# Down weights of the two convolution-hosting feed-forward stages split in two fp32r halves

## The chip, the cores and the metric

The kernel runs on one core of a Trainium2 chip, as one program. The metric is the device time of one execution in microseconds. A core has a matrix engine (TensorE, PE in the profile; PEld is its weight load), three engines for elementwise work (VectorE is DVE, ScalarE is ACT, GpSimd is POOL), and a queue that only starts transfers (SyncE, SP). Each engine works through its own list in order, and they meet at semaphores. "Start to start" is the time from the start of one instruction to the start of the next on the same engine; an instruction's own duration is a little longer, since neighbours overlap by 0.08 us.

## The reference

Two blocks in sequence on 256 tokens of width 1024, in fp32. The first has a mixer (gated linear attention and block attention), then a feed-forward layer whose depthwise convolution of three taps is causal. The second has two layers on a latent and a context sequence of 256 tokens each, modulated by projections of a condition vector: a conformer convolution of 31 taps with layer norm, and window attention. Each is followed by a feed-forward layer of this form:

```python
def conv_ffn(h, w_up, w_dw, b_dw, w_down):      # w_up 1024 x 5632, w_down 2816 x 1024
    u = dwconv(h @ w_up, w_dw, b_dw)            # three taps
    a, b = jnp.split(u, 2, axis=-1)
    return (jax.nn.silu(a) * b) @ w_down
...
    v = a * jax.nn.sigmoid(g)                   # conformer_conv
    v = dwconv(v, w_dw, b_dw)                   # 31 taps
    v = jax.nn.silu(layernorm(v, ln_g, ln_b))
    return v @ w_pw2 + b_pw2
```

## The kernel before

All weights lie in HBM as slabs of 128 x 2048 fp32 (1 MB), in the order of their use. A ring of three buffers `raw` takes them in; slab c is in slot c modulo 3, and since the order in a feed-forward stage repeats every three slabs, each of its three kinds keeps one slot. A product in nearly full precision is made of three fp32r matmuls (`mm3`, lines 1706 to 1708): the upper half of the weights `whi` with the upper and the lower half of the activations, and the lower half `wlo` with the upper half of the activations. For that, each slab is split:

- ScalarE writes `whi` as a copy of `raw` (`hi`, line 777). It waits until the slab has landed and until TensorE is through with the slab that last used the slot.
- VectorE and GpSimd write `wlo = raw - whi` together (`lo`, lines 1171 and 735). `pool_words` gives GpSimd's part: the last 512 columns in the stages of `DOWN_WHOLE`, else the last 1024. VectorE takes the rest.
- The next load into the slot waits for both parts.

Slabs that are kept `whole` skip this. TensorE reads them from `raw` as fp32 (line 626 for down weights, 1776 for the modulation), and the next load into the slot waits for TensorE. Before the change these are the modulation slabs and the down weights of `ffn0` and `ffn_ctx`.

There are four feed-forward stages: `ffn0`, `ffn_ctx`, `ffn_lat`, `ffn2`. Each walks over 11 blocks of 256 inner features (j = 0 to 10, called pairs here, for the pair of tap buffers). For each, TensorE does two up slabs, for the two halves of u (`features`), and one down slab for block j - 1 (`down`). For block j ScalarE applies the middle tap with the bias out of PSUM (`tap`, line 457) and silu (477). VectorE adds the other two taps out of PSUM (line 540, four instructions a half) and multiplies the halves (559, 512 columns). Where down weights are split, ScalarE then copies the product to `m_hi` (487) and VectorE subtracts `m_lo` (568), 512 columns each, before `down`.

`ffn0` and `ffn_ctx` host the 31-tap convolution of the conformer layer between these steps (`host`). ScalarE makes products of one tap with all eight tiles (871, 128 x 2048 in eight instructions, into `bufA` and `bufB` by turns), VectorE adds each to `acc`, which is the tile `sra` (1296, 128 x 2048), and does one tap in each block itself (1303, eight instructions). Blocks 2 to 7 have three products and one own tap each, blocks 0 and 1 two products and one own tap, block 8 the last addition. The layer norm follows in blocks 8 to 10.

The list of a block on VectorE is: lower half of the first up slab of block j + 1, taps of the first half, host step 0, lower half of the second up slab, taps of the second half, host step 1, multiplication, host step 2, and, where split, lower half of down slab j and m_lo. The end of each stage is drawn apart: behind down slab 9 stand three modulation slabs, then the last down slab (`ffn0_end` and the like), which goes to the slot of the first modulation slab and can be loaded only after that one is used. Then `outputs` waits for its banks, and VectorE adds them to the residual (1376, 1392 and 1550).

Of the kernel before, what the change touches and what calls it, by code (L numbers as in the profile page):

```python
# [31 lines left out]
RING = 3  # L32
# [137 lines left out]
PROCESSING = processing()  # L170


DOWN_WHOLE = {"ffn0", "ffn_ctx"}


def kept_whole():

    out = []
    for use, i in KEYS:
# [3 lines left out]
        elif use.startswith("ada"):  # L183
            out.append(True)
        elif ffn in DOWN_WHOLE:
            out.append(use != ffn or (i >= 4 and i % 3 == 1))
# [8 lines left out]

def pool_words(use):

    return 512 if use.removesuffix("_end") in DOWN_WHOLE else 1024


class Slab:
# [58 lines left out]
def build(nc, io):  # L260
# [16 lines left out]
    with ctx:  # L277
# [146 lines left out]
        def down_slab(b0, j):  # L424

            return b0 + 3 * j + 4
# [9 lines left out]
        def split_ffn(use):  # L436

            return [u for u in ("ffn0", "ffn_ctx", "ffn_lat", "ffn2") if u not in DOWN_WHOLE].index(use) if use not in DOWN_WHOLE else None

        def ffn_v(f):  # L440
            return (0, 1, 1, 2)[f]
# [4 lines left out]
        def ffn_act(act, hi, f, use, tail=None, host=None):  # L446

            b0, whole, fs = BASE[use], use in DOWN_WHOLE, split_ffn(use)
            centre = 2 if f == 0 else 1
            c, b = COL[f"ffn_w{ffn_v(f)}"][0] + centre * 2 * FT, COL[f"ffn_b{ffn_v(f)}"][0]  # L450

            def tap(half, j, par):

                buf = (cva, cvb)[half]
                for m in range(2):
                    t = 2 * j + (m + half * FT)
                    ins = act.activation(buf[:, par, m, :], ps[:, 2 * par + half, m * T:m * T + T], ACT.Identity,  # L457
                                         scale=cols[:, bass.ds(t + c, 1)], bias=cols[:, bass.ds(t + b, 1)])
                ins.then_inc(tap0, 1)

            def up(g, j, par, first):
                hi(g + RING)
                act.wait_ge(slab_done, g.number() + 1)
                if not first:
                    act.wait_ge(mid_f, j + (f * NJ - 1))
                tap(0, j, par)
                if host:
                    host(j, par, 0)
                hi(g + (RING + 1))
                act.wait_ge(slab_done, g.number() + 2)  # L470
                if not first and not whole:
                    act.wait_ge(mid_lo, j + (fs * NJ - 1))
                tap(1, j, par)
                if host:
                    host(j, par, 1)
                act.wait_ge(conv_out, 2 * j + (f * 2 * NJ + 1))
                act.activation(cva[:, par, :, :], cva[:, par, :, :], ACT.Silu).then_inc(silu_done, 1)
                if host:
                    host(j, par, 2)

            def split(j, par, first):
                if whole:
                    return
                act.wait_ge(mid_f, j + (f * NJ + 1))
                if not first:
                    act.wait_ge(slab_done, down_slab(b0, j - 2) + 1)
                act.activation(m_hi[:, par, :, :], cvb[:, par, :, :], ACT.Copy).then_inc(mid_hi, 1)

            up(Slab(b0), 0, 0, True)
            split(0, 0, True)  # L490
            up(Slab(b0 + 2), 1, 1, True)
            hi(Slab(b0 + 4 + RING))
            split(1, 1, True)
            if host:
                with act.Fori(0, 3) as jj:
                    for u in range(2):
                        up(Slab(b0 + 5 + 3 * u, 2, jj), 2 * jj + (2 + u), u, False)
                for j in (NJ - 3, NJ - 2):
                    up(Slab(b0 + 3 * j - 1), j, j % 2, False)
            else:  # L500
                with act.Fori(0, 4) as jj:
                    for u in range(2):
                        g = Slab(b0 + 5 + 3 * u, 2, jj)
                        up(g, 2 * jj + (2 + u), u, False)
                        hi(g + (2 + RING))
                        split(2 * jj + (2 + u), u, False)
            g = Slab(b0 + 3 * NJ - 4)
            up(g, NJ - 1, 0, False)
            others = BASE[use + "_end"] - BASE[use] - COUNT[use]
            hi(g + (2 + RING))  # L510
            if others == RING:
                hi(g + (3 + RING))
            split(NJ - 1, 0, False)
            for k in range(1 if others == RING else 0, others):
                hi(g + (3 + k + RING))
            if tail:
                tail()
            hi(g + (3 + others + RING))
            return g.c + 3 + others + RING + 1


        def ffn_dve(dve, lo, order, f, use, host=None, tail=None):

            b0, whole, fs = BASE[use], use in DOWN_WHOLE, split_ffn(use)

# [69 lines left out]
        def ffn_pe(pe, features, mm3, f, use, x, split, free, early=None, before_down=None, before_end=None, host=None):  # L595


            b0, whole, fs = BASE[use], use in DOWN_WHOLE, split_ffn(use)

# [122 lines left out]
        def _(pool):  # L722
# [4 lines left out]
            def run(c, use, k0, k1):  # L727

                part = slice(SLAB - pool_words(use), SLAB)

                def lo(g):
                    if g.whole:
                        return
                    pool.wait_ge(hi_done, g.split() + 1)
                    pool.tensor_tensor(wlo[:, g.slot, part], raw[:, g.slot, part], whi[:, g.slot, part].bitcast(F32),  # L735
                                       ALU.subtract).then_inc(lo2_done, 1)

                while k0 < k1 and not steady(c + k0, c + k1):
                    lo(Slab(c + k0))
                    k0 += 1  # L740
                times = (k1 - k0) // RING
                if times > 1:
                    with pool.Fori(0, times) as j:
                        for k in range(RING):
                            lo(Slab(c + k0 + k, 1, j))
                    k0 += RING * times
                for k in range(k0, k1):
                    lo(Slab(c + k))
# [18 lines left out]
        def _(act):  # L767
# [272 lines left out]
            def squares_after(q, x, ready):  # L1040
# [4 lines left out]
                return tail  # L1045

            c = ffn_act(act, hi, 0, "ffn0", squares_after(0, xlat, 4), conv_act(0, h_hi))


# [11 lines left out]
            gate_bias(1, xlat, 5 * KT)  # L1061
            pw1_act(1, PLACE["pw1_lat", 2], 5, xctx, ctx_sq, ctx_y, h_hi, shift_of(0, 3, 1), (x_ready, 12))
            c = ffn_act(act, hi, 1, "ffn_ctx", squares_after(1, xctx, 12), conv_act(1, g_hi))


# [14 lines left out]
            group_rows("ada_b")  # L1080
            c = hi_to(c, "ffn_lat", 2)
            c = ffn_act(act, hi, 2, "ffn_lat", lambda: squares(xlat, bufB, preload=True, ready=20))


# [77 lines left out]
        def _(dve):  # L1162
            order = Tally(dve_order)

            def lo(g):

                if isinstance(g.j, int) and g.c >= TOTAL or g.whole:
                    return
                part = slice(0, SLAB - pool_words(use_of(g.c)))
                dve.wait_ge(hi_done, g.split() + 1)  # L1170
                dve.tensor_tensor(wlo[:, g.slot, part], raw[:, g.slot, part], whi[:, g.slot, part].bitcast(F32), ALU.subtract)\  # L1171
                   .then_inc(lo_done, 1)
# [1090 lines left out]
```

## Time and profile before

| | |
|---|---|
| median of 3 runs | 1545.44 us (1545.22 to 1550.87) |
| profiled execution, first to last instruction | 1542.9 us, 2.5 us less than the median; the page gives no other time of it |
| TensorE busy | 1435.2 us, 93% |
| VectorE busy | 1006.8 us, 65% |
| ScalarE busy | 823.3 us, 53% |
| GpSimd busy | 580.9 us, 38% |
| mean granted TensorE clock | 0.968 of full speed |
| HBM read | 269.73 MB, 176 GB/s over the span |

The busy shares are means over stages with different limits. The two stages that the change touches run from about 377 to 592 us (`ffn0`) and from about 683 to 898 us (`ffn_ctx`). A busy TensorE includes the overlap of neighbouring matmuls, so its share says that it never rested, not that each matmul was at its shortest.

### The profile page before, as it was taken

The page shows a single profiled execution, that of the slowest core. Times are in us where ns is not written, and L with a number is a line of the kernel's source. Part 1 is how long each engine was busy: PE and PEld are TensorE (multiplying, and loading weights), DVE is VectorE, ACT ScalarE, POOL GpSimd, SP SyncE. Part 2 cuts the span into 40 slices and gives each one's busy share as a digit, 9 for nine tenths or more (in the row PEclk, how much of TensorE's full clock was granted, in tenths as well). Part 3 has the DMA queues.
Part 4 walks back from the last instruction along what each step waited for, and adds up shares of the span by engine and source line. Part 5 has one row for each costly group of instructions (what it writes and reads, how often), then busy time and mean ns, then how long its engine had stood idle before and what let it go on. Part 6 is the DMA issues. An engine that isn't in the chain of part 4 may idle for free.

```text
span 1542.9 us, 27912 instructions
## 1 busy us (share of the span) xinstructions
PE 1435.2 (93%) x11026; PEld 1325.8 (86%) x11026; DVE 1006.8 (65%) x1299; ACT 823.3 (53%) x1155; POOL 580.9 (38%) x192
## 2 busy tenths in 40 slices
PE   5999999899999999899999988999977998699996
PEld 3898879899999987799999878999966767599996
DVE  4322534747899967678999667666656763666666
ACT  3633454445888653558886545545523453355452
POOL 2443335355332213442222144565523300355662
PEclk9999999999999999999999989999988899899998
DMA  7775564345344446542444465555445300454550
GB/s 288 274 281 191 217 246 164 133 169 193 120 164 167 182 171 272 218 164 110 175 181 184 171 227 194 183 186 190 175 165 199 117 0 29 180 202 171 183 190 28
DMA packets 39142, 272.05 MB, mean 176 GB/s; under 512 B 4437, under 2 KB 5589, under 8 KB 6415
## 3 DMA queue, kind: packets, MB, share of 16 engines
q1 hardware_dynamic: 39054, 270.81, 47.2%
q8 instruction: 65, 1.06, 0.3%
q14 instruction: 23, 0.18, 0.0%
HBM read 269.73 MB, written 1.06 MB: 176 GB/s over the span
## 4 chain that ended last, share of the span: by engine, by line
PE 82%; DVE 8%; ACT 3%; DMA 3%; issue 2%; POOL 1%; SPq 0%; DVEq 0%; ACTq 0%; POOLq 0%
PE ps L1706 22%; PE ps L1707 21%; PE ps L1708 21%; PE ps L626 10%; DMA raw<-w_dram 3%; PE ps L1776 2%; DVE rstd L1180 2%; ACT whi L777 2%; PE ps L2068 1%; PE ps L2080 1%; DVE wlo L1171 1%; DVE h_lo L1220 1%; POOL wlo L735 1%; PE ps L1742 1%; DMA mv<-b_forget_dram 1%
## 5 line engine op out<-in xcount | busy, mean ns | idle before, releaser
L735 POOL TENSOR_TENSOR wlo<-raw,whi 128x1024 fp32r<-128x1024 f32 (+1 forms) x183 | 578.6, 3164 | 935.3 <-ACT whi L777 935.3
L777 ACT ACTIVATE whi<-raw 128x2048 fp32r<-128x2048 f32 x183 | 349.4, 1911 | 501.8 <-PE ps L1708 307.2
L1171 DVE TENSOR_TENSOR wlo<-raw,whi 128x1024 fp32r<-128x1024 f32 (+1 forms) x183 | 275.7, 1507 | 383.6 <-ACT whi L777 382.5
L1706 PE MATMUL ps<-h_hi,whi 128*128 128x256 f32 x1320 | 383.7, 291 | 23.0 <-DVE h_lo L1220 17.4
L1707 PE MATMUL ps<-h_lo,whi 128*128 128x256 f32 x1320 | 377.2, 286 | 0.0
L1708 PE MATMUL ps<-h_hi,wlo 128*128 128x256 f32 x1320 | 376.9, 285 | 0.0
L1706 PE MATMUL ps<-g_hi,whi 128*128 128x256 f32 x1088 | 313.6, 288 | 9.1 <-DVE g_lo L1220 2.5
L1707 PE MATMUL ps<-g_lo,whi 128*128 128x256 f32 x1088 | 309.5, 284 | 0.0
L1708 PE MATMUL ps<-g_hi,wlo 128*128 128x256 f32 x1088 | 309.4, 284 | 0.0
L1706 PEld LDWEIGHTS ps<-h_hi,whi 128*128 128x128 f32 x1320 | 256.3, 194 | 35.1 <-issue 29.1
L1707 PEld LDWEIGHTS ps<-h_lo,whi 128*128 128x128 f32 x1320 | 256.8, 195 | 0.4
L1708 PEld LDWEIGHTS ps<-h_hi,wlo 128*128 128x128 f32 x1320 | 256.7, 194 | 0.0
L1706 PEld LDWEIGHTS ps<-g_hi,whi 128*128 128x128 f32 x1088 | 210.3, 193 | 13.5 <-issue 5.0
L1707 PEld LDWEIGHTS ps<-g_lo,whi 128*128 128x128 f32 x1088 | 210.3, 193 | 0.4
L1708 PEld LDWEIGHTS ps<-g_hi,wlo 128*128 128x128 f32 x1088 | 210.1, 193 | 0.0
L626 PE MATMUL ps<-cvb,raw 128*128 128x256 f32 x704 | 160.8, 388 | 2.0 <-DMA raw<-w_dram 2.0
L626 PEld LDWEIGHTS ps<-cvb,raw 128*128 128x128 f32 x704 | 135.9, 195 | 21.9 <-DMA raw<-w_dram 3.3
L1706 PE MATMUL ps<-m_hi,whi 128*128 128x256 f32 x384 | 109.8, 286 | 9.3 <-DVE m_lo L568 9.3
L1707 PE MATMUL ps<-m_lo,whi 128*128 128x256 f32 x384 | 109.6, 285 | 0.0
L1708 PE MATMUL ps<-m_hi,wlo 128*128 128x256 f32 x384 | 109.5, 285 | 0.0
L540 DVE SCALAR_TENSOR_TENSOR cvb<-ps,cols,cvb 128x255 f32<-128x255 f32 (+1 forms) x176 | 76.6, 477 | 14.9 <-ACT cvb L457 10.3
L540 DVE SCALAR_TENSOR_TENSOR cva<-ps,cols,cva 128x255 f32<-128x255 f32 (+1 forms) x176 | 76.7, 477 | 10.9 <-ACT cva L457 6.2
(237 smaller groups left out, 1891.6 us busy)
## 6 DMA issues: line engine op xcount, KB each, us to landing
raw<-w_dram SPq DMA_DIRECT2D x253, 1024.0 KB, 4.9
xlat<-xT_dram SPq DMA_DIRECT2D x1, 1024.0 KB, 4.9
brev<-bias_rows SPq DMA_DIRECT2D x1, 1024.0 KB, 8.8
brev<-ctxT_dram SPq DMA_DIRECT2D x1, 1024.0 KB, 8.9
out_dram<-xlat SPq DMA_DIRECT2D x4, 256.0 KB, 2.5
cols<-cols_dram SPq DMA_DIRECT2D x1, 512.0 KB, 5.7
gates<-tables_dram SPq DMA_DIRECT2D x1, 448.0 KB, 5.7
consts<-consts_dram SPq DMA_DIRECT2D x1, 192.0 KB, 10.3
```

The costliest lines, as they stand in the source:

```text
L540: ins = dve.scalar_tensor_tensor(out, ps[:, 2 * par + half, m * T + src:m * T + src + n], w, out, ALU.mult, ALU.add)
L626: ins = pe.matmul(ps[:, 4 + m // 2, (m % 2) * T:(m % 2) * T + T], wf[:, k, m * P:m * P + P], cvb[:, par, k, :], start=(first and k == 0 an ...
L735: pool.tensor_tensor(wlo[:, g.slot, part], raw[:, g.slot, part], whi[:, g.slot, part].bitcast(F32), ALU.subtract).then_inc(lo2_done, 1)
L777: act.activation(whi[:, g.slot, :], raw[:, g.slot, :], ACT.Copy).then_inc(hi_done, 1)
L1171: dve.tensor_tensor(wlo[:, g.slot, part], raw[:, g.slot, part], whi[:, g.slot, part].bitcast(F32), ALU.subtract)\
L1180: dve.tensor_reduce(rstd[:, i, :], sq[:, 1024 * i:1024 * i + 1024].rearrange("p (t n) -> p n t", n=T), AX.X, ALU.add)\
L1220: ins = dve.scalar_tensor_tensor(out[1][:, m, :], y[:, m * T:m * T + T], shift(m), out[0][:, m, :].bitcast(F32), ALU.add, ALU.subtract)
L1706: pe.matmul(out, w[0], x[0], start=start, stop=False, skip_group_check=True)
L1707: pe.matmul(out, w[0], x[1], start=False, stop=False, skip_group_check=True)
L1708: return pe.matmul(out, w[1], x[0], start=False, stop=stop, skip_group_check=True)
L1742: ins = pe.matmul(ps[:, bank, 0:T], ones[:, :], s, start=(i == 0), stop=(i == len(sums) - 1))
L1776: ins = pe.matmul(ps[r:r + QUAD, bank, 0:SLABC], cnd[:, c:c + QUAD], w[:, t, :], start=(t < 4 and k == 0), stop=(t >= 4 and k == n - 1), s ...
```

## The change

`DOWN_WHOLE` becomes empty. Then `whole` is false for the down slabs of `ffn0` and `ffn_ctx`; ScalarE, VectorE and GpSimd split them as in the other two stages, `down` takes its three-matmul branch, m_hi and m_lo are made there too, and loads into these slots wait for the two lower halves and no more for TensorE. `pool_words` is 1024 for every slab. In ScalarE's loop of the hosting stages the upper half of the down slab and m_hi (`split`) are put behind the host's last step of each block. VectorE's and TensorE's functions have the split branch already.

```diff
-DOWN_WHOLE = {"ffn0", "ffn_ctx"}
+DOWN_WHOLE = set()
...
 def pool_words(use):
 
-    return 512 if use.removesuffix("_end") in DOWN_WHOLE else 1024
+    return 1024
...
             if host:
                 with act.Fori(0, 3) as jj:
                     for u in range(2):
-                        up(Slab(b0 + 5 + 3 * u, 2, jj), 2 * jj + (2 + u), u, False)
+                        g = Slab(b0 + 5 + 3 * u, 2, jj)
+                        up(g, 2 * jj + (2 + u), u, False)
+                        hi(g + (2 + RING))
+                        split(2 * jj + (2 + u), u, False)
                 for j in (NJ - 3, NJ - 2):
-                    up(Slab(b0 + 3 * j - 1), j, j % 2, False)
+                    g = Slab(b0 + 3 * j - 1)
+                    up(g, j, j % 2, False)
+                    hi(g + (2 + RING))
+                    split(j, j % 2, False)
```

## Rows read from the trace of the kernel before

**Rows 1.** Page: busy by engine; shares of the chain that ended last.

```profile
PE 1435.2 (93%) x11026; PEld 1325.8 (86%) x11026; DVE 1006.8 (65%) x1299; ACT 823.3 (53%) x1155; POOL 580.9 (38%) x192
...
PE 82%; DVE 8%; ACT 3%; DMA 3%; issue 2%; POOL 1%; SPq 0%; DVEq 0%; ACTq 0%; POOLq 0%
PE ps L1706 22%; PE ps L1707 21%; PE ps L1708 21%; PE ps L626 10%; DMA raw<-w_dram 3%; PE ps L1776 2%; DVE rstd L1180 2%; ACT whi L777 2%; PE ps L2068 1%; PE ps L2080 1%; DVE wlo L1171 1%; DVE h_lo L1220 1%; POOL wlo L735 1%; PE ps L1742 1%; DMA mv<-b_forget_dram 1%
```

**Rows 2.** Groups by form: count, busy us, mean ns of one, idle before.

```profile
L777 ACT ACTIVATE whi<-raw 128x2048 fp32r<-128x2048 f32 x183 | 349.4, 1911 | 501.8 <-PE ps L1708 307.2 <-DMA raw<-w_dram 194.5
...
L626 PE MATMUL ps<-cvb,raw 128*128 128x256 f32 x704 | 160.8, 388 | 2.0 <-DMA raw<-w_dram 2.0
...
L568 DVE TENSOR_TENSOR m_lo<-cvb,m_hi 128x512 fp32r<-128x512 f32 x22 | 56.9, 2587 | 2.1 <-ACT m_hi L487 2.1
...
L487 ACT ACTIVATE m_hi<-cvb 128x512 fp32r<-128x512 f32 x22 | 13.6, 618 | 4.6 <-DVE cvb L559 4.6
```

**Rows 3.** Windows of one pair: ffn0, ffn_ctx, ffn_lat; length, busy by engine, clock, DMA.

```profile
437.20:455.61 18.41, 18.41 (x129) 17.59 (x129) 17.44 (x23) 15.81 (x33) 5.77 (x3) 1.00 0.43 171
780.16:798.57 18.41, 18.41 (x129) 17.59 (x129) 17.85 (x23) 15.26 (x31) 4.18 (x3) 1.00 0.44 171
1000.00:1017.28 17.28, 17.28 (x146) 17.28 (x146) 10.71 (x14) 8.60 (x9) 10.33 (x4) 1.00 0.51 183
```

**Rows 4.** Timeline of one pair in ffn0, VectorE, then GpSimd: start, us, instruction, idle before.

```profile
490.53 1.76 DVE L1171 TENSOR_TENSOR wlo<-raw,whi 128x1536 fp32r<-128x1536 f32 x1 [0.29 <-ACT whi L777]
492.20 1.88 DVE L540 SCALAR_TENSOR_TENSOR cva<-ps,cols,cva 128x254 f32<-128x254 f32 x4
494.00 2.28 DVE L1296 TENSOR_TENSOR sra<-sra,bufB 128x2048 f32<-128x2048 f32 x1
496.42 1.76 DVE L1171 TENSOR_TENSOR wlo<-raw,whi 128x1536 fp32r<-128x1536 f32 x1
...
505.64 0.68 DVE L559 TENSOR_TENSOR cvb<-cva,cvb 128x512 f32<-128x512 f32 x1
506.24 2.28 DVE L1296 TENSOR_TENSOR sra<-sra,bufB 128x2048 f32<-128x2048 f32 x1
508.82 1.76 DVE L1171 TENSOR_TENSOR wlo<-raw,whi 128x1536 fp32r<-128x1536 f32 x1 [0.30 <-ACT whi L777]
...
490.57 2.86 POOL L735 TENSOR_TENSOR wlo<-raw,whi 128x512 fp32r<-128x512 f32 x1 [9.53 <-ACT whi L777]
```

**Rows 5.** Timeline at a down slab of ffn_lat, VectorE, then GpSimd.

```profile
1014.44 1.23 DVE L1171 TENSOR_TENSOR wlo<-raw,whi 128x1024 fp32r<-128x1024 f32 x1 [1.72 <-ACT whi L777]
1015.59 2.89 DVE L568 TENSOR_TENSOR m_lo<-cvb,m_hi 128x512 fp32r<-128x512 f32 x1
...
1014.49 3.44 POOL L735 TENSOR_TENSOR wlo<-raw,whi 128x1024 fp32r<-128x1024 f32 x1 [2.31 <-ACT whi L777]
```

**Rows 6.** Timeline at a first up slab of ffn_ctx, VectorE, then GpSimd.

```profile
758.37 2.28 DVE L1296 TENSOR_TENSOR sra<-sra,bufA 128x2048 f32<-128x2048 f32 x1
760.57 1.75 DVE L1171 TENSOR_TENSOR wlo<-raw,whi 128x1536 fp32r<-128x1536 f32 x1
...
759.88 3.57 POOL L735 TENSOR_TENSOR wlo<-raw,whi 128x512 fp32r<-128x512 f32 x1 [8.41 <-ACT whi L777]
```

**Rows 7.** Chain that ended last: one down slab and the end of ffn0.

```profile
400.37 6.91 PE ps L626 x32
...
575.34 7.12 DMA raw<-w_dram
...
582.51 9.18 PE ps L626 x32
```

**Rows 8.** Timeline of the end of ffn_lat, ScalarE, then VectorE.

```profile
1139.38 1.91 ACT L777 ACTIVATE whi<-raw 128x2048 fp32r<-128x2048 f32 x1 [10.14 <-DMA raw<-w_dram]
...
1142.47 2.83 DVE L568 TENSOR_TENSOR m_lo<-cvb,m_hi 128x512 fp32r<-128x512 f32 x1
...
1153.38 0.88 DVE L1392 SCALAR_TENSOR_TENSOR xlat<-ps,mod,xlat 128x256 f32<-128x256 f32 x2 [0.56 <-PE ps L1708]
```

## The prediction

> **What bounds the kernel now.** I began with the busy shares and the chain that ended last [rows 1]: TensorE is 93% busy and 82% of the chain, so in most stages a saving in its work shows in the time, unless another engine is about as full. The table by groups gives the two prices that the change swaps [rows 2]: a down slab kept whole runs as 704 / 22 = 32 matmul instructions, and in the chain each slab stands as one piece of 6.91 us [rows 7]; a split slab is 48 matmuls. Windows one period long show the stage as a whole [rows 3]. In ffn0 and ffn_ctx a pair (two up slabs and one down slab) takes 18.41 us, in ffn_lat, where all slabs are split, 17.28. TensorE is full in all three windows, so a split down slab costs 17.28 / 3 = 5.76 us, 1.15 less than 6.91. The same rows carry the warning: VectorE is busy 10.7 us of 17.28 in ffn_lat, but 17.44 and 17.85 us of 18.41 in the stages that host the convolution. There two engines are full. The convolution's additions make the difference, and the change puts more work on just that engine.
>
> VectorE's queue over one pair is listed in [rows 4]: from one first subtraction (490.53) to the next (508.82) 18.29 us. It waits twice for ScalarE's upper half. A queue without waits starts an instruction 0.08 us before the last one ends; measured so the waits are 0.38 and 0.22 us. 17.7 us are work, and no rest of note is left.
>
> **The change part by part.** *TensorE*: minus 1.15 us for each of 22 down slabs, 25 us busy in all, if nothing else sets the pace.
>
> *ScalarE*: one more slab copy, 1.8 us from start to start, and one more m_hi copy, about 0.55 us, on 15.8 busy us per pair [rows 2, 3]: 18.2 us. That is above the 17.28 that TensorE would like, below what VectorE comes to, and it costs nothing beside it.
>
> *VectorE*: the subtraction of 1536 columns takes 1.67 us of its queue (490.53 to 492.20), that of 1024 takes 1.15 (1014.44 to 1015.59) [rows 4, 5]. Two of the first, 3.34, become three of the second, 3.45. The m_lo subtraction of 512 columns is new: 0.60, the place that the multiplication of the same shape takes between 505.64 and 506.24. 17.7 + 0.1 + 0.6 = 18.4 us, with no wait for anyone.
>
> *GpSimd*: two subtractions of 512 columns become three of 1024. It has the time (three in ffn_lat are 10.33 busy us of 17.28 [rows 3]). What matters is what it does to VectorE. In [rows 5] both begin a subtraction at 1014.44 and 1014.49. VectorE ends at 1015.67 and GpSimd at 1017.93, that is 2.26 us later; where m_lo is behind, it stands as 2.89 us, where the multiplication of the same shape takes 0.68, and ends 0.55 us after GpSimd. So the two take turns when both read two operands of SBUF: 512 columns on GpSimd hold VectorE off for some 1.14 us (490.57 + 2.86 less 492.29), 1024 for 2.26. The tap accumulation is free of this. It reads PSUM, and it runs at its normal 1.88 us while GpSimd works [rows 4]. Today both GpSimd pieces, 1.14 us each, disappear wholly under the 1.80 us of taps. With 1024 columns each overhangs: 2.26 + 0.09 - 1.80 = 0.55 us that the addition behind the taps must wait, 1.1 for two. The third piece, that of the down slab, has no taps behind it but an m_lo, as in ffn_lat. Whoever it falls on, VectorE stands still about 2.3 us. 18.4 + 1.1 + 2.3 = 21.8 us per pair.
>
> That holds if the three pieces find the two tap windows. If one of the two misses it (the additions are 2.2 us each, three in a pair, and a piece that meets an addition's end takes the next 2.3 us), it is 18.4 + 2 x 2.3 + 0.55 = 23.6. Between them the order at each hand-over decides, and the trace shows both answers. In [rows 5] GpSimd waited and got the next turn, ahead of m_lo. In [rows 6] GpSimd asked at 759.88, the addition ended at 760.65, and VectorE's next subtraction went first all the same: 3.57 us instead of 2.86. The Trainium skill ("SBUF — State Buffer", Who interferes with whom) says that a VectorE instruction with two SBUF inputs and a GpSimd instruction that reads SBUF exclude each other for the whole instruction, and that issue order decides who blocks. By that order GpSimd would have had its turn at 760.65, and the pair would go to the 23.6 side; the row contradicts it once VectorE has a run of such instructions behind it. I take the middle, 22.7 us, 4.3 more than 18.41.
>
> *How many pairs*: a stage has 11. Pairs 2 to 7 have the full load (three additions, one own tap): 6 x 4.3 = 26 us, by the ends 20 to 31. Pairs 0 and 1 have fewer additions (one and two) beside an own tap: VectorE's list for pair 1 is 18.4 - 2.2 + 2.9 to 5.2 = 19 to 21 us, and pair 0 starts behind the first taps: I take 4.5 us for both. Pairs 8 to 10 have one addition and the layer norm, VectorE rests there today, and TensorE's shorter down slabs count at last: 3 x 1.15 = 3.5 us at most, of which I take 1, for they begin with VectorE behind. Three loads of the next mod slabs and the short waits between are unchanged.
>
> *The end of the stage*: the last down slab's load waits for the mod slab before it and lands 7.12 us after TensorE has nothing else to do; TensorE then starts at once and takes 9.18 us instead of 6.91 after the pause [rows 7]. Split, it needs the upper half, the lower half and m_lo first. ffn_lat shows just this: from the start of the upper half (1139.38, at landing) over m_lo to the last output drained 1153.38, 14.0 us [rows 8]. 14.0 - 9.2 = 4.8 us; the end in ffn_ctx looks alike and I take 4.5 for each.
>
> *What moves otherwise*: a raw slab of down weights is now freed when its halves are made and not when TensorE is through, so loads come earlier. Each is hidden: at 171 to 183 GB/s the queues have room [rows 3]. m_hi and m_lo are free, two pairs apart. The number of bytes is the same.
>
> *Sum*: 4.5 + 26 - 1 + 4.5 = 34 us per stage, 68 for two; by the ends 28 and 39, 56 to 78. The profiled span is 1542.9 us, 2.5 under the median of 1545.44, and the difference is carried over as it is. TensorE would stand still some 5 us in each pair; before, it was slower after a pause (9.18 for 6.91). In the loop it has that time to spare, at the pairs behind I add 1 us. **1545 + 69 = 1614 us.**
>
> **The rivals.**
> *TensorE's saving wins (faster).* VectorE would have to do its pair in 17.3 us. Then 10 x 1.15 = 11.5 us less and 4.5 more at the end of each stage: 1531 us. For it: TensorE is the larger share of the chain, and VectorE rests in pairs 8 to 10. Against: the queue alone is 18.4 us, and the subtractions stand in it in front of work that TensorE waits for, so it can fall behind by one pair only. It decides from the point where VectorE and GpSimd overlap wholly and some 1.1 us of VectorE's list goes.
> *The engines overlap after all.* If GpSimd held VectorE off only where it does now, the pair is 18.4 to 18.8 us. The period stays, the ends cost 4.5 and pairs 0 to 7 up to 3: 1545 + 9 to 15 = about 1557 us. Against it speak all m_lo in ffn_lat and ffn2, 2.6 us in the mean [rows 2].
> *No window is found.* All three pieces fall on additions or subtractions: 18.4 + 6.9 = 25.3 us per pair, 6 x 6.9 = 41 us, with 4.5 + 4.5 and 1 for the two first pairs about 51 per stage: 1647 us. For it: once VectorE is late, upper halves are ready long before it comes to them, and GpSimd starts when it likes.
> *TensorE slows with its pauses* so far that it sets the pace again. At the stretch that [rows 7] show after a pause it takes 9.18 / 6.91 = 1.33 times as long; a whole pair so is 17.28 x 1.33 = 23.0 us, inside the forecast's own span, and only a longer slow stretch would lie above it. It is in the upper tail.
>
> **How the numbers follow.** The forecast (VectorE and GpSimd by turns, one or two pieces uncovered) 0.81; no window or a slow TensorE 0.10; overlap after all 0.06; TensorE's saving 0.03. The forecast's own range is 1601 to 1625; with late starts of the pairs, the hand-overs and a part of the upper rival 1592 to 1640. About 0.5%, 8 us, is what a measurement of this kernel can tell from no change: faster 0.03, same 0.02, slower 0.95.
>
> **What would show it.** In the pairs 2 to 7: 21.8 to 23.6 us from one first subtraction to the next, TensorE busy 17.3 of them, with its waits put down to VectorE's m_lo or GpSimd's wlo; the additions behind the taps longer than 2.28 us. m_lo far above 0.68 us in all four stages. 205 instead of 183 subtractions on GpSimd, all of 1024 columns. About 14 us from the landing of the end slab to its last output. A pair of 17.3 us in ffn0 would make the prediction wrong at its root; one of 18.5 would say that the turns cost nothing; one of 25 that no window is found. A period of ScalarE without rest would mean that I blamed the wrong engine.

## The result and the profile after

The change made the kernel slower: 1593.35 us median (1589.06 to 1595.71, 4 runs) against 1548.02 us of the kernel before beside it, ratio 1.0298 with a 95% interval of 1.0277 to 1.0319. The profiled execution has a span of 1587.3 us, 44.4 more than 1542.9. The forecast was 1614 us, with a range of 1592 to 1640: the right way and mechanism, but half as large again as the growth that came, 69 us against 45. Line numbers behind the changed function are 6 higher (1706 is 1712, 1296 is 1302).

The page, where it answers to [rows 1]: busy time by engine, then the chain that ended last.

```profile
PE 1424.8 (90%) x11378; PEld 1336.2 (84%) x11378; DVE 1081.2 (68%) x1343; ACT 873.8 (55%) x1199; POOL 720.7 (45%) x214
...
PE 61%; DVE 12%; issue 11%; ACT 8%; POOL 4%; DMA 2%; ACTq 1%; SPq 0%; DVEq 0%; POOLq 0%
```

TensorE is busy 10 us less and its share of the chain falls from 82% to 61%. What came in its place are VectorE, ScalarE and GpSimd, and "issue", from 2% to 11%, which is time for which the profile names no wait. The groups by form, which answer to [rows 2]: count, busy us and mean ns, idle before and who ended it.

```profile
L741 POOL TENSOR_TENSOR wlo<-raw,whi 128x1024 fp32r<-128x1024 f32 x205 | 718.4, 3512 | 840.0 <-ACT whi L783 840.0
...
L1712 PE MATMUL ps<-m_hi,whi 128*128 128x256 f32 x736 | 219.3, 298 | 75.2 <-DVE m_lo L574 36.1 <-POOL wlo L741 31.8 <-issue 7.3
...
L574 DVE TENSOR_TENSOR m_lo<-cvb,m_hi 128x512 fp32r<-128x512 f32 x44 | 76.3, 1734 | 3.5 <-ACT m_hi L487 3.5
```

TensorE's waits stand before the first matmul of a down slab, for m_lo and for GpSimd's lower half, 75.2 us in all. In windows of one period, one in ffn0 and one in ffn_ctx, which answer to [rows 3]:

```profile
484.65:506.00 21.35, 17.50 (x126) 17.33 (x125) 20.78 (x26) 18.01 (x34) 13.78 (x4) 0.84 0.42 147
791.90:813.25 21.35, 19.79 (x166) 19.59 (x165) 20.79 (x25) 17.95 (x34) 13.78 (x4) 1.00 0.42 147
```

A pair now takes 21.35 us. VectorE is full (20.8; the rest are its own 0.27 us between an addition and the own tap, and 0.14 us twice between taps). ScalarE is busy 18.0, near the 18.2 of the forecast. TensorE rests before each down slab; the two windows cut its work at different places, so its 17.5 and 19.8 us are not its share of a pair. In the first window it waited 3.85 us before the down slab and took 8.39 us for it, and the granted clock is 0.84 in the mean; in the second the wait was 1.56 us, the slab took 6.01, and the clock stayed at 1.00. VectorE's queue over one pair, under it one row of ScalarE, then GpSimd's, answer to [rows 4]:

```profile
502.01 0.69 DVE L565 TENSOR_TENSOR cvb<-cva,cvb 128x512 f32<-128x512 f32 x1
502.62 2.29 DVE L1302 TENSOR_TENSOR sra<-sra,bufA 128x2048 f32<-128x2048 f32 x1
504.82 1.22 DVE L1177 TENSOR_TENSOR wlo<-raw,whi 128x1024 fp32r<-128x1024 f32 x1
505.95 0.69 DVE L574 TENSOR_TENSOR m_lo<-cvb,m_hi 128x512 fp32r<-128x512 f32 x1
506.56 1.22 DVE L1177 TENSOR_TENSOR wlo<-raw,whi 128x1024 fp32r<-128x1024 f32 x1
507.69 1.89 DVE L546 SCALAR_TENSOR_TENSOR cva<-ps,cols,cva 128x254 f32<-128x254 f32 x4
509.50 2.67 DVE L1302 TENSOR_TENSOR sra<-sra,bufB 128x2048 f32<-128x2048 f32 x1
512.17 3.34 DVE L1177 TENSOR_TENSOR wlo<-raw,whi 128x1024 fp32r<-128x1024 f32 x1
515.44 1.88 DVE L546 SCALAR_TENSOR_TENSOR cvb<-ps,cols,cvb 128x254 f32<-128x254 f32 x4
517.23 2.70 DVE L1302 TENSOR_TENSOR sra<-sra,bufA 128x2048 f32<-128x2048 f32 x1
...
523.38 0.69 DVE L565 TENSOR_TENSOR cvb<-cva,cvb 128x512 f32<-128x512 f32 x1
...
510.24 1.90 ACT L783 ACTIVATE whi<-raw 128x2048 fp32r<-128x2048 f32 x1
...
503.99 13.79 POOL L741 TENSOR_TENSOR wlo<-raw,whi 128x1024 fp32r<-128x1024 f32 x3 [7.57 <-ACT whi L783]
```

Read the durations. Three instructions are longer than their kind: the two additions behind taps, 2.67 and 2.70 instead of 2.28, and the subtraction at 512.17, 3.34 instead of 1.22. Together 0.39 + 0.42 + 2.12 = 2.93 us, and 18.4 + 2.9 = 21.3. GpSimd asks at 503.99. VectorE runs the rest of its addition, a subtraction, m_lo and another subtraction before the turn passes at 507.78, at the first taps, 3.8 us later. So m_lo is not held up here (0.69). GpSimd's row holds three pieces, which start in the trace at 503.99, 509.98 and 514.39: those of the down slab, of the first and of the second up slab. The first runs under the first taps, the second takes its whole turn before the subtraction at 512.17, the third runs under the second taps.

Not all of the 2.93 us is the turns' own price. ScalarE's upper half of the second up slab ends at 512.14, and the addition at 512.17: without the overhang of 0.39 VectorE would have waited there for ScalarE. The kernel with 32 columns below has just that wait.

The end of ffn0 in the chain that ended last; it answers to [rows 7], and to the end of ffn_lat in [rows 8]:

```profile
594.60 1.05 PE ps L1782 x16
595.66 5.01 DMA raw<-w_dram
600.70 1.92 ACT whi L783
602.64 1.23 DVE wlo L1177
603.87 2.77 DVE m_lo L574
606.63 0.14 issue
```

The last down slab ends at 614.31 (before 591.69). With the multiplications (line 559, now 565) as marks, the 44 us divide so: ffn0 22.6 us, the stretch between the stages 0.9, ffn_ctx 23.0, and 2.1 given back behind it, 1.4 of them by the third pair of ffn_lat.

### The profile page after: what moved, and what is told of

Its sections match the earlier page's. It is cut to its first block, busy times and chain, and to the rows that moved or that the text cites. A ratio compares the mean times of both kernels' runs of the same rounds, so it can differ in the third digit from the quotient of the medians.

```text
span 1587.3 us, 28890 instructions
## 1 busy us (share of the span) xinstructions
PE 1424.8 (90%) x11378; PEld 1336.2 (84%) x11378; DVE 1081.2 (68%) x1343; ACT 873.8 (55%) x1199; POOL 720.7 (45%) x214
## 4 chain that ended last, share of the span: by engine, by line
PE 61%; DVE 12%; issue 11%; ACT 8%; POOL 4%; DMA 2%; ACTq 1%; SPq 0%; DVEq 0%; POOLq 0%
PE ps L1712 18%; PE ps L1713 17%; PE ps L1714 17%; POOL wlo L741 4%; ACT whi L783 3%; DMA raw<-w_dram 2%; PE ps L1782 2%; DVE rstd L1186 2%; DVE wlo L1177 2%; DVE sra L1302 1%; ACT bufA L877 1%; PE ps L2086 1%; PE ps L2074 1%; DVE h_lo L1226 1%; ACT bufB L877 1%
## 5 line engine op out<-in xcount | busy, mean ns | idle before, releaser
L741 POOL TENSOR_TENSOR wlo<-raw,whi 128x1024 fp32r<-128x1024 f32 x205 | 718.4, 3512 | 840.0 <-ACT whi L783 840.0
L783 ACT ACTIVATE whi<-raw 128x2048 fp32r<-128x2048 f32 x205 | 391.2, 1910 | 460.4 <-PE ps L1714 327.4
L1177 DVE TENSOR_TENSOR wlo<-raw,whi 128x1024 fp32r<-128x1024 f32 x205 | 312.9, 1528 | 356.6 <-ACT whi L783 356.1
L1712 PE MATMUL ps<-m_hi,whi 128*128 128x256 f32 x736 | 219.3, 298 | 75.2 <-DVE m_lo L574 36.1
L1712 PEld LDWEIGHTS ps<-m_hi,whi 128*128 128x128 f32 x736 | 150.3, 204 | 79.6 <-issue 74.7
L1713 PE MATMUL ps<-m_lo,whi 128*128 128x256 f32 x736 | 216.6, 294 | 0.0
L1714 PE MATMUL ps<-m_hi,wlo 128*128 128x256 f32 x736 | 216.3, 294 | 0.0
L1713 PEld LDWEIGHTS ps<-m_lo,whi 128*128 128x128 f32 x736 | 150.2, 204 | 0.1
L1714 PEld LDWEIGHTS ps<-m_hi,wlo 128*128 128x128 f32 x736 | 149.9, 204 | 0.0
```

The lines of the kernel that those rows point to most:

```text
L783: act.activation(whi[:, g.slot, :], raw[:, g.slot, :], ACT.Copy).then_inc(hi_done, 1)
L1712: pe.matmul(out, w[0], x[0], start=start, stop=False, skip_group_check=True)
L1713: pe.matmul(out, w[0], x[1], start=False, stop=False, skip_group_check=True)
L1714: return pe.matmul(out, w[1], x[0], start=False, stop=stop, skip_group_check=True)
```

## The experiments

Each is compared with the kernel before on the same chip. A period is the distance of two multiplications in blocks 2 to 7. Spans of single executions also differ ahead of the change: the first multiplication of ffn0 stands between 395 and 407 us. Where that matters, the stretch from this mark to the first multiplication of ffn_lat is given, which is 568.4 us in the kernel before and 613.5 with the change.

**GpSimd at 512 columns, down slabs split.**

```diff
-    return 1024
+    return 512 if use.removesuffix("_end") in ("ffn0", "ffn_ctx") else 1024
```

> The change with GpSimd at 512 columns in the two hosting stages (ffn0, ffn_ctx), down slabs split as in the change. Theory A (VectorE's own list sets the period, and GpSimd adds what its pieces overhang): VectorE's list grows by 3 x 0.52 to about 19.9 us, two pieces of 1.14 us must share one tap window of 1.8 us, about 0.6 us over, so 20.5 us per pair instead of 21.35; span about 1587 - 11 = 1576 us. Rival B (only the total that GpSimd does counts, not VectorE's columns): the blocked time halves and the period is 18.4 + 1.4 = 19.8 us, span 1566. Rival C (VectorE's columns alone count): 19.9 + 2.9 = 22.8 us, span over 1600.

Measured: 1591.05 us, ratio 1.0282 (1.0257 to 1.0307), span 1591.2, period 21.57 us. All three theories missed. VectorE's timeline of one pair:

```profile
488.51 1.88 DVE L546 SCALAR_TENSOR_TENSOR cva<-ps,cols,cva 128x254 f32<-128x254 f32 x4
490.30 2.80 DVE L1302 TENSOR_TENSOR sra<-sra,bufA 128x2048 f32<-128x2048 f32 x1
493.03 2.84 DVE L1177 TENSOR_TENSOR wlo<-raw,whi 128x1536 fp32r<-128x1536 f32 x1
495.79 1.88 DVE L546 SCALAR_TENSOR_TENSOR cvb<-ps,cols,cvb 128x254 f32<-128x254 f32 x4
```

The list is the 19.95 us that were expected, and the overhang behind the first taps is 0.52, where about 0.6 was. What theory A left out is a whole turn, 2.84 instead of 1.75, before the subtraction of the second up slab: 19.95 + 0.52 + 1.09 = 21.56. GpSimd's piece for that slab was asked for during the addition and took its end instead of the taps behind. So what VectorE gains by a larger share of GpSimd's, it pays back in turns: 18.4 + 2.9 or 19.95 + 1.6.

**GpSimd at 1024 columns, down slabs whole.**

```diff
-    return 512 if use.removesuffix("_end") in DOWN_WHOLE else 1024
+    return 1024
```

> The kernel before, with GpSimd at 1024 columns of each slab in the hosting stages and the down slabs kept whole. Theory A: VectorE's list shrinks by 2 x 0.52 us and gains up to 0.4 us behind each tap window, 17.4 us, under TensorE's 18.41; so the period stays 18.41 and the time is that of before within 3 us. Rival (the larger piece of GpSimd is what costs, with or without the down slab): the period rises by 2 x 0.4 to 2.1 us and the time by 12 us or more.

Measured: ratio 1.001 (0.9995 to 1.0026), span 1543.9, periods 18.3 to 18.5 us in ffn0 and 18.5 in the mean in ffn_ctx (17.4 to 19.8). Theory A. The larger share alone costs nothing as long as TensorE sets the pace; the loss is the split's.

**GpSimd's turns taken away.**

```diff
+                if use.removesuffix("_end") in ("ffn0", "ffn_ctx"):
+                    part = slice(SLAB - 32, SLAB)
```

The 992 columns before them are left out, so this kernel does less work than it should, and only its times count.

> The change, but in the hosting stages GpSimd subtracts only the last 32 columns of each slab and leaves the 992 before them as they are (part of the lower halves is left out); VectorE's part stays 1024. Theory A (turns with GpSimd make 2.9 us of the 21.35): the period falls to VectorE's own list, 18.4 to 18.7 us, and the span by 2 x 6 x 2.8 = 34 us, to about 1553. Rival (ScalarE's list of 18.0 busy us with its waits for products, or the loads, set 21.35): the period stays above 20.5 and the span above 1578.

Measured, in one execution: span 1551.9 us, period 18.82. Window of one period (length, then busy PE, PEld, DVE, ACT, POOL, granted clock, DMA share, GB/s):

```profile
482.78:501.60 18.82, 18.36 (x153) 18.08 (x151) 17.86 (x26) 17.97 (x34) 5.39 (x4) 1.00 0.43 167
```

Theory A: with GpSimd's part of the work and nothing else taken out, 2.5 us of the period go and 35 us of the span; from mark to mark 41 us go (572.3 for 613.5), since this execution reached ffn0 5.8 us later. 0.41 of the 18.82 us is a wait for ScalarE's upper half. The rival, ScalarE or the loads at 21.35, is out for the kernel as it stands, but ScalarE is close behind: of the 2.93 us of turns 0.4 only stand in the place of this wait. What is left over 18.41 shows that even with hardly any turns the hosting stages would gain nothing from the split (572.3 against 568.4).

**VectorE's share of the convolution made light, split and whole.**

```diff
-                dve.tensor_tensor(flat(acc[:, :, :]), flat(acc[:, :, :]), buf[:, :], ALU.add)...
+                dve.tensor_tensor(flat(acc[:, 0:4, :]), flat(acc[:, 0:4, :]), buf[:, 0:1024], ALU.add)...
...
-                    ... dve.scalar_tensor_tensor(acc[:, t, :], vpad[:, t, bass.ds(k, T)], w, acc[:, t, :], ...)
+                    ... dve.scalar_tensor_tensor(acc[:, t, 0:32], vpad[:, t, bass.ds(k, 32)], w, acc[:, t, 0:32], ...)
```

> The change with VectorE's part of the hosted convolution made light: each addition covers half the columns (1024 of 2048) and each own tap 32 of 256 columns, so part of the convolution is left out. Theory A (TensorE's saving is real and is only buried under VectorE's list): the list falls by 3 x 1.07 + 2.6 us to 12.6, with GpSimd's turns to about 15.5, under 17.28; TensorE sets the pace at 17.28 us per pair, and the time is that of before less 2 x (10 x 1.15 - 2.3) = 18 us, about 1527. Rival (ScalarE's 18.0 busy us are next in line): the period is 18 us or more and the time 1538 or more.

> The kernel before with the same light convolution (half additions, own taps of 32 columns; part of the convolution left out). Theory A: TensorE sets 18.41 us per pair already, so the time stays at that of before within 3 us. Rival (VectorE shares the pace of before): several us less.

Measured: whole, ratio 0.9999 (0.9981 to 1.0017), as theory A has it. Split, 1569.2 us, ratio 1.0143 (1.0123 to 1.0164), period 21.18 us. Here theory A fell, and the rival's words fit the number but not its reason, since ScalarE is not full either. VectorE, then ScalarE, in the split kernel:

```profile
485.35 1.21 DVE L1177 TENSOR_TENSOR wlo<-raw,whi 128x1024 fp32r<-128x1024 f32 x1
486.49 1.88 DVE L546 SCALAR_TENSOR_TENSOR cvb<-ps,cols,cvb 128x254 f32<-128x254 f32 x4
...
494.86 1.23 DVE L1177 TENSOR_TENSOR wlo<-raw,whi 128x1024 fp32r<-128x1024 f32 x1 [1.93 <-ACT whi L783]
496.01 2.85 DVE L574 TENSOR_TENSOR m_lo<-cvb,m_hi 128x512 fp32r<-128x512 f32 x1
498.78 3.42 DVE L1177 TENSOR_TENSOR wlo<-raw,whi 128x1024 fp32r<-128x1024 f32 x1
...
503.92 2.71 DVE L1302 TENSOR_TENSOR sra<-sra,bufB 128x1024 f32<-128x1024 f32 x1
...
485.60 3.31 ACT L877 ACTIVATE bufA<-gates,cols 128x256 f32 x8 [2.82 <-DVE sra L1302]
488.81 0.62 ACT L477 ACTIVATE cva<-cva 128x512 f32<-128x512 f32 x1
489.72 3.31 ACT L877 ACTIVATE bufB<-gates,cols 128x256 f32 x8 [0.30 <-DVE sra L1302]
492.94 1.90 ACT L783 ACTIVATE whi<-raw 128x2048 fp32r<-128x2048 f32 x1
```

VectorE now has waits of its own (1.93 us before 494.86), so its list no longer sets the pace. A circle over two engines does: from the end of an addition (485.4) two products, silu and the down slab's upper half on ScalarE to 494.84, then VectorE's subtraction, m_lo and the next subtraction, with two whole turns of GpSimd in them (2.85 and 3.42), then taps and the addition again, which waits for a third piece (2.71 for 1.22), to 506.6, 21.2 us later. Since VectorE and GpSimd start on the down slab together again, m_lo pays the turn, as in [rows 5].

**The same with GpSimd's turns taken away, and then with light products.** The first puts the edit of the 32 columns on the light split kernel, the second lets ScalarE make half of each product as well:

```diff
-                for t in range(KT):
+                for t in range(KT // 2):
                     w = cols[:, bass.ds(KT * k + (COL["dw_w"][0] + t), 1)]
```

> e4 (split, VectorE's additions and own taps light) with GpSimd's part of each slab in the hosting stages cut to its last 32 columns as well; parts of the convolution and of the lower halves are left out. Theory A (in e4 a loop over two engines holds 21.2 us: from an addition over ScalarE's two products and the upper half of the down slab to VectorE's subtractions, which wait for two whole turns of GpSimd, to the taps and back to the addition): without the turns, 2 x 2.2 + 0.5 = 4.9 us go, the loop is 16.3 us, and ScalarE's own list of 17.9 us is next: 17.9 to 18.3 us per pair. Rival (the loop is ScalarE and its products, GpSimd has no part): the period stays above 20.5.

> e9 with ScalarE's products for four of eight tiles only (half of each product is left out too). Theory A: ScalarE's list falls by 3 x 1.6 us, TensorE is the next bound, 17.28 us per pair, so each split down slab gives its 1.15 us; span about 1543 - 2 x (10 x 1.15 - 2.3) = 1525. Rival (something else than the three engines, as loads or waits for a buffer, keeps the pair above 18): the span stays above 1535.

Measured, in one execution each: spans 1521.5 and 1518.3 us, periods 17.85 and 17.28. A window of the first, a little shorter than its period, then one of the second:

```profile
440.00:457.50 17.50, 17.50 (x148) 17.50 (x147) 12.87 (x24) 17.50 (x34) 3.88 (x3) 1.00 0.47 180
```

```profile
480.00:497.28 17.28, 17.28 (x146) 17.28 (x145) 13.07 (x25) 13.39 (x21) 3.88 (x3) 1.00 0.50 182
```

ScalarE is full in the first, and its list is the period. TensorE is full there too, but it works off what it is behind: its down slabs start 17.28 us apart (433.76, 451.04, 468.32), the multiplications 17.85, and it first waits again at 520.76, for m_lo. In the second only TensorE is full. Both are theory A. The saving of 1.15 us per down slab is real, and three things lie over it: VectorE's list with GpSimd's turns (21.35), the circle (21.2), and ScalarE's list (17.85).

**The end slab kept whole.**

```diff
-        elif use.startswith("ada"):
+        elif use.startswith("ada") or use in ("ffn0_end", "ffn_ctx_end"):
             out.append(True)
...
+                whole = last and use in ("ffn0", "ffn_ctx")
                 if whole:
```

> The change, with only the last down slab of ffn0 and ffn_ctx kept whole. Theory A (at the end of a stage the chain of upper half, lower half and m_lo behind the landing costs 4.5 us against a whole slab, and the earlier landing after a split stage gives some 2 back): 3.5 to 4.5 us less per stage than the change, 7 to 9 in all, ratio to before 1.024. Rival (the end costs the 2.3 us net that the profile shows, and the early landing goes with the split slab): 4 to 5 us less in all.

Measured: 1584.14 us, ratio 1.0234 (1.0216 to 1.0253), span 1580.0, 7.3 less than the change; by the marks the two stage ends take 3.8 and 4.2 us less. The end of ffn0 in its chain:

```profile
597.57 4.77 DMA raw<-w_dram
602.38 10.22 PE ps L633 x32
```

Theory A: the chain over the lower halves costs 13.6 us from the landing (600.70 to 614.31) against 10.2 here. The load takes 4.77 us, and 5.01 in the change, against 7.12 before [rows 7]. The end slab is whole here and its load is as short, so that gain belongs to the split slabs ahead.

**GpSimd only 32 columns of the down slabs.**

```diff
-def pool_words(use):
-
+def pool_words(c):
+
+    use, i = KEYS[c]
+    if use in ("ffn0", "ffn_ctx") and i >= 4 and i % 3 == 1:
+        return 32
     return 1024
```

> The change, with GpSimd taking only 32 columns of each down slab in the loops of the hosting stages and VectorE the other 2016; the up slabs keep 1024. Theory A (it is the third piece, the one without a tap window, that costs a whole turn): VectorE's list grows by 1.03 to 19.4, the two pieces of the up slabs overhang 0.4 each, 20.3 us per pair instead of 21.35, span 1587 - 12 = 1575. Rival (columns weigh the same wherever they are, as e1 suggests): the period stays at 21.3 to 21.6 us.

Measured: 1600.71 us, ratio 1.0342 (1.0312 to 1.0372), period 22.18 us. Theory A missed, and so did the rival. VectorE's timeline:

```profile
492.32 0.69 DVE L577 TENSOR_TENSOR m_lo<-cvb,m_hi 128x512 fp32r<-128x512 f32 x1
492.93 1.22 DVE L1179 TENSOR_TENSOR wlo<-raw,whi 128x1024 fp32r<-128x1024 f32 x1
494.06 1.89 DVE L549 SCALAR_TENSOR_TENSOR cva<-ps,cols,cva 128x254 f32<-128x254 f32 x4
495.86 2.89 DVE L1304 TENSOR_TENSOR sra<-sra,bufA 128x2048 f32<-128x2048 f32 x1
498.67 3.40 DVE L1179 TENSOR_TENSOR wlo<-raw,whi 128x1024 fp32r<-128x1024 f32 x1
502.00 1.88 DVE L549 SCALAR_TENSOR_TENSOR cvb<-ps,cols,cvb 128x254 f32<-128x254 f32 x4
503.79 2.28 DVE L1304 TENSOR_TENSOR sra<-sra,bufB 128x2048 f32<-128x2048 f32 x1
```

The third piece is gone and the whole turn is still there, 3.40 us at 498.67. Now the second up slab's piece pays it: GpSimd asked at 497.54, while the addition ran, and the second taps (502.00) passed with nobody to use them; the addition behind is 2.28. The list and the turns add up: 19.4 + 0.6 + 2.2 = 22.2. So "the one without a tap window" was wrong as a reason. Here, in the change and with 512 columns, the piece that pays whole is the one that GpSimd asks for, or still waits with, while VectorE is in the addition behind the first taps: the second up slab's here and with 512 columns, the first up slab's in the change.

**Only late down slabs split.** Blocks 8 and 9 of each hosting stage, then the same with 1024 columns for GpSimd, then block 7 too (for which blocks 6 and 7 are drawn out of the loops). The edit of the first, in part:

```diff
+LATE = (8, 9)
...
-            out.append(use != ffn or (i >= 4 and i % 3 == 1))
+            out.append(use != ffn or (i >= 4 and i % 3 == 1 and (i - 4) // 3 not in LATE))
```

> The kernel before, with only the down slabs of blocks 8 and 9 split in each hosting stage, used where VectorE has little of the convolution left; 512 columns for GpSimd as before. Theory A: TensorE sets the pace there, so each split slab gives its 1.15 us: 4 x 1.15 = 4.6 us less, ratio 0.997. Rival (VectorE's layer-norm steps, behind the new subtractions, set the pace there): no change or up to 4 us more.

> Down slabs of blocks 8 and 9 split as in e6, and 1024 columns for GpSimd in the hosting stages, so VectorE's list in the loop is 1 us shorter and its subtractions in blocks 8 to 10 too. Theory A: the loop stays at TensorE's 18.41 us, the late blocks give the 4.6 us: ratio 0.997, as e6 or 1 us better. Rival (GpSimd's longer turns hit the steps of the layer norm): worse than e6, ratio 1.000 or more.

> As e8 (1024 columns for GpSimd in the hosting stages, late down slabs split), with block 7 split as well as 8 and 9. Theory A: its down slab is used behind pair 8, where VectorE has some room, and gives another 1.15 us per stage: 2 us less than e8, ratio 0.994. Rival (its m_lo and lower half lie in a pair that still has the full convolution, and what VectorE is late by moves the layer norm): as e8 or slower.

Measured: 1543.8 us, ratio 0.9979 (0.9961 to 0.9997); 1542.02 us, ratio 0.9951 (0.9934 to 0.9968); 1542.41 us, ratio 0.9975 (0.996 to 0.999). The best beats both kernels, by half a per cent at most. Its profiled span is only 1 us under that of the kernel before (1541.9 against 1542.9), but it reached ffn0 5 us later (402.5 against 397.3), ahead of anything that was changed. From mark to mark the three take 564.3, 564.2 and 564.2 us against 568.4, so 4 us go, near the 4.6 of theory A; these are single executions, and the other kernels with whole down slabs stand at 570 to 571. Splitting is worth its price where VectorE has little else to do, and block 7 adds nothing that shows in the medians.

## Why the prediction was right, and where it was off

**The number.** 1593.35 us lies in the range of 1592 to 1640 by 1.4 us, and under the forecast's own 1601 to 1625. That it lies inside is partly luck: the forecast added its growth to 1545.44, while the kernel before beside the result has 1548.02; with the first, the same growth of 45 us would give 1591. What the experiments bear out is the mechanism.

**TensorE.** A split down slab costs 5.8 us against 6.9, and where nothing lies over it (the light kernel) the pair is 17.28 us. In the change it bought nothing in blocks 0 to 7.

**ScalarE.** 18.2 us was said, 18.0 measured, and it does not set the pace. It is closer to doing so than the text let see: in each pair its upper half of the second up slab comes just as VectorE ends the addition (512.14 and 512.17), and with VectorE light and hardly any turns it sets the pace, at 17.85.

**VectorE's list.** 18.4 us was said. The rows give 21.35 less 2.93 of turns, 18.4, and the kernel without turns 18.82 less a wait of 0.41.

**The turns.** This is the term that was mis-sized. I put the pair at 21.8 or 23.6 us and took the middle, 22.7; it is 21.35, so six pairs at 4.3 us were too many. From the multiplication of block 2 to that of block 8 the growth is 16.3 us in ffn0 and 16.0 in ffn_ctx, against 26. Two steps of it failed. Taking the middle between the two answers at a hand-over was wrong: VectorE kept its turn at each hand-over inside a run, as in [rows 6], and lost just the one behind taps and a single addition. With that the down slab's piece did find a tap window, so the sign "m_lo far above 0.68 us in all four stages" failed in the hosting loops (0.69). And the piece that pays the whole turn isn't the down slab's by its nature, as the kernel with 32 columns of the down slabs shows; the count of one whole turn and two overhangs held all the same, at 2.12 and twice 0.4 us, 2.9 in all against the 3.4 of the low end.

**The order of the turns.** By issue order alone GpSimd, which asked at 503.99, would have run at the end of the addition at 504.9; it ran at 507.78. The exclusion that the Trainium skill ("SBUF — State Buffer", Who interferes with whom) states is borne out by every whole turn here, its order is not: at 512.17 the piece that had waited since 509.98 did go first, at 504.9 the one that had waited since 503.99 did not.

**The first pairs.** 4.5 us was said; measured 6.2 in ffn0 (2.35 until the multiplication of block 0, 3.8 to that of block 2) and 5.7 in ffn_ctx.

**The last pairs.** 1 us less was said, and it is 1.0 less in ffn0 and 0.3 in ffn_ctx.

**The end of the stage.** 4.5 us was said, and from the multiplication of block 10 it is 1.1 and 1.6. The price of the chain was right (13.6 us from the landing for 9.2 before; 3.8 and 4.2 us by the kernel with a whole end slab), but "Each is hidden", said of the loads that come earlier, was not: here is the one that isn't hidden. It took 2.1 us less, 5.01 for 7.12, and it began 1.2 us sooner behind the multiplication of block 10: 4.4 - 2.1 - 1.2 = 1.1 us in ffn0.

So the stage, 34 us in the forecast, is 6.2 + 16.3 - 1.0 + 1.1 = 22.6 in ffn0 and 5.7 + 16.0 - 0.3 + 1.6 = 23.0 in ffn_ctx. Of the rivals, "no window" came near on no pair, and "the engines overlap" is refuted by the 32-column kernel, 35 us faster. TensorE's pauses did lower its clock (0.84 in a window). Since it had time to spare there, no cost of that is to be seen in a period: four down slabs in a row take 8.39, 5.99, 7.49 and 5.99 us and start 21.3 us apart all the same (488.79, 510.12, 531.47, 552.79).

What stays open is why the turn passes at one hand-over and not at another. The traces show a pattern. In all twelve pairs of blocks 2 to 7 of the change GpSimd asked in the middle of an addition that had not itself waited, and VectorE kept its turn at the three hand-overs behind it; the addition behind the first taps had itself waited for GpSimd, and the turn passed behind it, twelve times out of twelve. Taps are not needed for that: in the light kernel m_lo had waited (2.85 us at 496.01), and the subtraction behind it paid the next turn. Whether the earlier wait is the cause was not tested.

## What to carry to other kernels

Before lightening the engine with the largest share, list the queue of the second engine over one period, start to start; if it has no rest, a saving on the first buys nothing, and each instruction added to the second is paid in full. Where VectorE and GpSimd both read two operands of SBUF, as here, count GpSimd's work as VectorE's time, except for what falls under instructions that read PSUM or in place of another wait. A part of such a change can still pay in the blocks where the second engine rests, and behind each removed bound the next one should be looked for before the gain is counted.

## What the runs showed of the hardware

A VectorE run of two-operand instructions without a gap held GpSimd off for 3.8 us over four instructions (503.99 to 507.78), while behind taps out of PSUM and one addition the waiting GpSimd went ahead of the next subtraction, in each of the twelve pairs of blocks 2 to 7 (periods 21.30 to 21.37 us). Half the columns on GpSimd, or 32 for one slab of three, did not shorten the period (21.57 and 22.18 us): the turn only moved to another slab.
